# A decoder layer on one core: the recurrence in chunks of 64 tokens instead of 32

## The chip, the core and the metric

One NeuronCore of a Trainium2 chip runs the whole layer in one launch. The metric is device time in microseconds (us), the median of several executions. A profile is one execution, taken by the hardware profiler. Engines are called as the profile calls them: PE (TensorE, the matrix products; PEld its weight loads), DVE (VectorE), ACT (ScalarE), POOL (GpSimd) and SP (SyncE, which here issues most of the DMAs; ACT issues the others).

## What is computed

One hybrid layer on 2048 tokens of width 1024, all in float32. The token mixer has a projection, then two groups of heads: an RWKV-7 recurrence (8 heads of 64) and causal pooling; then an output projection, norms, and a gated MLP with a causal convolution. The part that the change rewrites is the recurrence:

```python
def step(state, inp):
    r_t, w_t, k_t, v_t, a_t, b_t = inp
    sa = jnp.einsum('bhvk,bhk->bhv', state, a_t)
    state = (state * w_t[:, :, None, :] + sa[..., None] * b_t[:, :, None, :]
             + v_t[..., None] * k_t[:, :, None, :])
    y_t = jnp.einsum('bhvk,bhk->bhv', state, r_t)
    return state, y_t
...
_, y = lax.scan(step, s0, seq)          # a = -kk, b = kk * alpha, per head 64 x 64 state
# then, per head: y = (y - mean) * rsqrt(var + eps) * ln_x_w + ln_x_b;  (y + bonus) * g
```

## The kernel before

The kernel has three phases. `phase_project` (lines up to L1020) forms the projection for four blocks of 512 tokens, scales r, k, a, b by the decay sums and stores them feature-major to scratch tensors in HBM; it also stores v and a token-major (`rows`, L899, sixteen 128x128 transposes a block, which `a_rows` at L609 copies and stores for a). In float32 it forms the grams of a and b inside chunks of C = 32 tokens and solves the inverse of (1 - strict gram) for two of the four blocks on DVE. `phase_recur` (L1024) runs the recurrence. `phase_out_and_ffn` and the output products do the rest of the layer.

`phase_recur` takes 128 tokens in an iteration `i`, from -2 to 19, with N = 16 groups of 128 tokens. It is a software pipeline written out by hand: `stages(i)` says which stages run in an iteration, `a1` for group i+2, `a2` for i+1, `b` for i, `o` for i-1, `c` for i-2, `d` for i-3. Each engine has its own `body(i, ...)`, whose order of instructions is the order in which that engine works; it stops at the first one whose semaphore isn't there. What stands in them:

- The chain, stage `b`, four times in an iteration, once for each chunk of 32 tokens: `from_state` (L1673, 4 products 128x64 by the state), ACT copies u from PSUM (`read_u`, L1402), `to_state` (L1681, 8 products), and DVE adds it to the state (`advance`, L1553; L1556 and L1559 in every second chunk, which also applies the decay `chunk_decay`). The next `from_state` waits for it.
- Preparation, `a1` and `a2`, for the groups to come: POOL builds `bk` from b and k (L1353, eight copies of 64x256, b and k interleaved and zeros between); `grams` (L1717, 32 products of 128x64); DVE masks them (`masks`, L1565, two instructions of 128x1024); `bk_transposes` (L1706, 16, copied by ACT at L1392); `z0_products` (L1729, 16 of 64x64), `w_products` (L1747, 32 of 32x32, from the inverse and from a token-major) and `z` (L1666, 16).
- Output, `o`: `from_r` (L1694, 32 products of 64x32) and `from_uv` (L1702, 32 of 128x32) into `ybank`, copied by ACT (L1472).
- Group norm, `c`: on DVE a sum, its scaling, a subtraction of the mean, the sum of squares, a reciprocal and a product (L1592, L1594, L1596, L1615, L1625, L1627); ACT squares (L1459) and takes the root (L1469). Stage `d`: four transposes (L1781), four scalings on ACT (L1446), bonus and gate on POOL (L1367, L1369), store.
- The inverses of the third and fourth block are solved in the gaps of DVE's order: `gap(0)` to `gap(7)` each take 2 to 4 small instructions (L1509, L1511), 27 parts a block over four iterations, the first part a mask of 128x1024 (L1500). This goes on in iterations 0 to 7 and is called solving below; iterations 8 to 15 have none of it.
- SP issues the loads of an iteration, 64 to 256 KB each: b and k, a and r, four of v, four of a, four of the inverse's 32x32 blocks (`spread`, L1222), bonus and gate.

PE has 228 products and transposes in a full iteration. Its order in it is: `from_state(0)`, `bk_transposes(0)`, `to_state(0)`, `from_r(0)`, the y transposes, `from_state(1)`, and so on to `w_products`, `grams` and `z`.

## Time and profile before

| what | value |
|---|---|
| median of 3 runs | 2328.89 us (2323.8 to 2330.03) |
| profiled execution, its span | 2329.1 us |
| PE busy | 2231.0 us, 96% |
| DVE, ACT, POOL busy | 1756.5, 1141.8, 1025.4 us |
| phase_project, first to last PE instruction | 0 to 541.6 us |
| phase_recur: first gram to `from_state(0)` of iteration 0 | 549.5 to 568.4 us |
| phase_recur: iterations 0 to 14 | 568.4 to 819.8 us |
| phase_recur: rest and change of phase | 819.8 to about 861 us |
| output products and MLP | about 861 to 2329 us |

A row of instructions reads: start, duration, engine, line of the kernel, operation, output<-input, shape, count, and in brackets how long the engine had been idle and for whom it waited. A float32 product is two records, so `x16` is eight products; a transpose is one record. "128*64 128x64" is a weight tile of 128 rows and 64 columns and an output of 64 columns moved through it.

### The profile page before, as it was taken

The page shows a single profiled execution, that of the slowest core. Times are in us where ns is not written, and L with a number is a line of the kernel's source. Part 1 is how long each engine was busy: PE and PEld are TensorE (multiplying, and loading weights), DVE is VectorE, ACT ScalarE, POOL GpSimd, SP SyncE. Part 2 cuts the span into 40 slices and gives each one's busy share as a digit, 9 for nine tenths or more (in the row PEclk, how much of TensorE's full clock was granted, in tenths as well). Part 3 has the DMA queues.
Part 4 walks back from the last instruction along what each step waited for, and adds up shares of the span by engine and source line. Part 5 has one row for each costly group of instructions (what it writes and reads, how often), then busy time and mean ns, then how long its engine had stood idle before and what let it go on. Part 6 is the DMA issues. An engine that isn't in the chain of part 4 may idle for free.

```text
span 2329.1 us, 43634 instructions
## 1 busy us (share of the span) xinstructions
PE 2231.0 (96%) x16652; PEld 1816.6 (78%) x16652; DVE 1756.5 (75%) x1910; ACT 1141.8 (49%) x1795; POOL 1025.4 (44%) x726
## 2 busy tenths in 40 slices
PE   7999999996999979998999999999999999999998
PEld 6777777775878768887888888788788888887886
DVE  3756798994884466769989999666799898976565
ACT  5646556452445554444444444454554444444543
POOL 4636466571234335535776766100146555541000
PEclk9999999998999989999999999999999999999999
DMA  7364556347567547895434343677733332326774
GB/s 203 93 227 134 178 160 209 106 140 216 154 166 194 144 144 234 268 279 166 153 119 147 121 146 128 217 252 255 237 119 115 104 111 93 113 95 202 247 260 145
DMA packets 435819, 395.61 MB, mean 170 GB/s; under 512 B 59548, under 2 KB 352076, under 8 KB 432332
## 3 DMA queue, kind: packets, MB, share of 16 engines
q1 hardware_dynamic: 407804, 343.06, 47.8%
q10 hardware_dynamic: 27856, 50.34, 6.0%
q8 instruction: 111, 1.82, 0.3%
q14 instruction: 48, 0.39, 0.1%
HBM read 266.97 MB, written 126.35 MB: 169 GB/s over the span
## 4 chain that ended last, share of the span: by engine, by line
PE 55%; DVE 3%; DMA 2%; ACT 1%; issue 1%; SPq 0%; ACTq 0%; POOLq 0%; POOL 0%; DVEq 0%
PE late_bank L133 18%; PE late_bank L134 18%; PE late_bank L135 18%; DVE wt_lo L2906 1%; DMA scratch_a<-p_keep 1%; ACT wt_hi L2727 1%; PE late_bank L2199 1%; DMA o_lo<-scratch_q 0%; DVE wt_lo L2860 0%; DMA p_keep<-in_w_down 0%; DMA raw<-in_w_down 0%; DMA scratch_x<-x_tile 0%; DMA p_keep<-scratch_td 0%; DVE p_ub L2869 0%; DVE x_tile L2168 0%
## 5 line engine op out<-in xcount | busy, mean ns | idle before, releaser
L133 PE MATMUL late_bank<-o_hi,wt_hi 128*128 128x512 f32 x1232 | 481.3, 391 | 8.0 <-DVE o_lo L2962 3.3
L134 PE MATMUL late_bank<-o_lo,wt_hi 128*128 128x512 f32 x1232 | 480.7, 390 | 0.0
L135 PE MATMUL late_bank<-o_hi,wt_lo 128*128 128x512 f32 x1232 | 480.6, 390 | 0.0
L431 POOL TENSOR_TENSOR p_w_lo<-p_w_raw,p_w_hi 128x1024 fp32r<-128x1024 f32 x72 | 190.4, 2645 | 221.2 <-ACT p_w_hi L502 221.2
L133 PEld LDWEIGHTS late_bank<-o_hi,wt_hi 128*128 128x128 f32 x1232 | 232.0, 188 | 58.7 <-issue 7.2
L135 PEld LDWEIGHTS late_bank<-o_hi,wt_lo 128*128 128x128 f32 x1232 | 232.1, 188 | 48.8
L134 PEld LDWEIGHTS late_bank<-o_lo,wt_hi 128*128 128x128 f32 x1232 | 232.0, 188 | 47.8
L2597 POOL TENSOR_TENSOR tsum<-raw 128x512 f32<-128x512 f32 x43 | 106.2, 2469 | 358.5 <-DVE p_ub L2947 179.4
L133 PE MATMUL p_ppr<-p_hT_hi,p_w_hi 128*128 128x512 f32 x576 | 233.4, 405 | 0.2 <-ACT p_ring L513 0.2
L133 PE MATMUL late_bank<-wt_hi 128*128 128x512 f32 x572 | 223.2, 390 | 7.2 <-DVE wt_lo L2906 6.6
L135 PE MATMUL p_ppr<-p_hT_hi,p_w_lo 128*128 128x512 f32 x576 | 226.6, 393 | 0.0
L134 PE MATMUL p_ppr<-p_hT_lo,p_w_hi 128*128 128x512 f32 x576 | 226.5, 393 | 0.0
L135 PE MATMUL late_bank<-wt_hi,wt_lo 128*128 128x512 f32 x572 | 222.6, 389 | 0.0
L134 PE MATMUL late_bank<-wt_lo,wt_hi 128*128 128x512 f32 x572 | 222.6, 389 | 0.0
L2674 ACT ACTIVATE wt_hi<-tsum 128x512 fp32r<-128x512 f32 x172 | 107.4, 627 | 169.3 <-PE late_bank L135 165.2
L2906 DVE TENSOR_TENSOR wt_lo<-raw,wt_hi 128x1024 fp32r<-128x1024 f32 x96 | 121.3, 1265 | 90.9 <-ACT wt_hi L2727 90.5
L2869 DVE TENSOR_TENSOR p_ub<-late_bank,p_ub 128x512 f32<-128x512 f32 x220 | 150.2, 683 | 34.6 <-PE late_bank L135 33.3
L2860 DVE TENSOR_TENSOR wt_lo<-raw,wt_hi 128x512 fp32r<-128x512 f32 x130 | 153.5, 1181 | 28.8 <-ACT wt_hi L2674 28.7
L2727 ACT ACTIVATE wt_hi<-raw 128x1024 fp32r<-128x1024 f32 x96 | 101.6, 1061 | 116.0 <-PE late_bank L135 96.9
L2860 DVE TENSOR_TENSOR wt_lo<-tsum,wt_hi 128x512 fp32r<-128x512 f32 x173 | 153.3, 887 | 1.8 <-ACT wt_hi L2674 0.6
L133 PEld LDWEIGHTS p_ppr<-p_hT_hi,p_w_hi 128*128 128x128 f32 x576 | 109.2, 190 | 36.3 <-issue 12.7
L133 PEld LDWEIGHTS late_bank<-wt_hi 128*128 128x128 f32 x572 | 107.4, 188 | 32.4 <-issue 6.4
(328 smaller groups left out, 4679.3 us busy)
## 6 DMA issues: line engine op xcount, KB each, us to landing
raw<-in_w_up SPq DMA_DIRECT2D x88, 512.0 KB, 5.1
p_w_raw<-in_w_in SPq DMA_DIRECT2D x72, 512.0 KB, 3.9
scratch_a<-p_keep SPq DMA_DIRECT2D x22, 1280.0 KB, 4.5
raw<-scratch_a SPq DMA_DIRECT2D x96, 256.0 KB, 3.0
raw<-scratch_td SPq DMA_DIRECT2D x52, 256.0 KB, 3.7
p_keep<-scratch_a SPq DMA_DIRECT2D x47, 256.0 KB, 2.9
scratch_a<-p_keep SPq DMA_DIRECT2D x44, 256.0 KB, 2.0
raw<-in_w_down SPq DMA_DIRECT2D x44, 256.0 KB, 4.1
```

Of the source, the lines that this page charges most:

```text
L133: nc.tensor.matmul(out, lhs_hi, rhs_hi, start=start, stop=False, skip_group_check=again)
L134: nc.tensor.matmul(out, lhs_hi, rhs_lo, start=False, stop=False, skip_group_check=again)
L135: return nc.tensor.matmul(out, lhs_lo, rhs_hi, start=False, stop=stop, skip_group_check=again)
L431: nc.gpsimd.tensor_tensor(w_lo[i][:, :, :], w_raw[i][:, :, :], w_hi[i][:, :, :].bitcast(F32), ALU.subtract).then_inc(s_wl, 1)
L2199: last = nc.tensor.transpose(bank[:, 4 + 2 * p + k // 4, (k % 4) * P:(k % 4 + 1) * P], hx[p][:, k * P:(k + 1) * P], ident[:, :])
L2597: nc.gpsimd.tensor_tensor(T1, B12, B11, ALU.subtract).then_inc(s_t, 1)
L2674: nc.scalar.activation(wt_hi[:, ph, :, :], weights(p, ph), ACT.Copy).then_inc(s_uh, 1)
L2727: nc.scalar.activation(dn_hi[r], dn_raw[r], ACT.Copy).then_inc(s_dh, 1)
L2860: nc.vector.tensor_tensor(wt_lo[:, ph, :, :], weights(p, ph), wt_hi[:, ph, :, :].bitcast(F32), ALU.subtract).then_inc(s_ul, 1)
L2869: nc.vector.tensor_tensor(dst, bank[:, b, :], src, ALU.add).then_inc(s_cd, 1)
L2906: nc.vector.tensor_tensor(dn_lo[r], dn_raw[r], dn_hi[r].bitcast(F32), ALU.subtract).then_inc(s_dl, 1)
```

## The change

C stays 32 for the grams that are inverted, but the recurrence goes over chunks of L = 64 tokens, two in an iteration.

- A chunk's step becomes: `from_state` (8 products 64x64 onto p in PSUM, where `z` has put the part of v), ACT copies p in two halves of four heads (`take_p`), `inverse` (8 products 64x64 by the 64x64 inverse, two halves, each as its half of p is there), ACT copies u in two halves (`take_u`), `to_state` (8 products 128x64), `advance` (two DVE instructions of 128x256).
- The 64x64 inverse is put together from the two 32x32 blocks and a corner: X21 = X2 L21 X1. `corner_left` and `corner_right` are 16 products of 32x32 each; a DVE transpose of 32x512 (`x1u`) and three kinds of ACT copies (`take_corner`, `m1`, `x21`) go with them. `w_products`, `z0_products`, the token-major a and its loads are gone, and in `phase_project` `a_rows`, its transposes and stores.
- b and k are stored and loaded as one tensor (`bk`), a and r (`ar`), bonus and gate (`bg`) likewise; POOL's copies (L1353) and its memset go. In an iteration SP issues 17 loads instead of 18: four of `bk` in pieces of 256 bytes, `ar`, v, `bg`, and ten of the inverse.
- PE: 156 products and transposes in a full iteration: `from_state` 16, `grams` 16 (64x128, 128 columns), `inverse` 16, `from_r` 16, y 4, `to_state` 16, corners 32, `transposed` 8, `from_uv` 16, `z` 16.
- `grams(c2)` fill both gram banks, so `grams(1)` waits for DVE's masks of `grams(0)` (`masked`, two instructions, 64x512 and 128x512, for each c2).
- Group norm: the subtraction of the mean, the square and the product by the reciprocal root move to POOL, which then has five instructions of 128x512 an iteration in place of two and eight copies. The root moves to the end of ACT's order, behind `x21`.
- The inverses are solved in six gaps an iteration over five iterations a block (27 parts as before), so in iterations 0 to 9; iterations 4 and 9 have only gaps 0 to 2.

The core of the diff; first DVE's order:

```diff
+                    if c:
+                        n = i - 2
+                        dve.wait_ge(s_yr, ONE + n + 1)
+                        nc.vector.tensor_reduce(stat[p][:, 0, :], y[n % 3][:, :, :], AX.X, ALU.add).then_inc(s_gn, 1)
+                        dve.wait_ge(s_gn, ONE + n + 1)
+                        nc.vector.tensor_scalar(stat[p][:, 0, :], stat[p][:, 0, :], -1.0 / H, None, ALU.mult).then_inc(s_mean, 1)
                     if a2:
-                        masks(am[q], strict, 0, s_am)
+                        n = i + 1
+                        dve.wait_ge(s_xl[n % 2], ONE + (n // 2 + 1) * 160)
+                        if n:
+                            wait_full(dve, i - 1, "m1")
+                        nc.vector.transpose(x1u[:, :, :, :].rearrange("p c u s -> p (c u s)"), x1[n % 2][:, :, :, :].rearrange("p c u t -> p (c u t)")
+                                            ).then_inc(s_xu, 1)
                     gap(0)
+                    gap(1)
...
+                    if a2:
+                        masked(0)
                     if b:
                         advance(0)
                     if a2:
-                        masks(ark[slot], causal, C, s_gr)
-                    gap(1)
...
+                        masked(1)
...
+                    gap(2)
...
+                    if c:
+                        dve.wait_ge(s_sq, ONE + i - 1)
+                        nc.vector.tensor_reduce(stat[p][:, 1, :], y2[:, :, :], AX.X, ALU.add).then_inc(s_var, 1)
+                    gap(3)
+                    if b:
+                        if o:
+
+                            dve.wait_ge(s_yd, ONE + 3 * (i - 1) + 2)
+                        advance(1)
                     gap(4)
                     if c:
-                        dve.wait_ge(s_sq, ONE + i - 1)
-                        nc.vector.tensor_reduce(stat[:, 1, :], y2[:, :, :], AX.X, ALU.add).then_inc(s_var, 1)
+                        dve.wait_ge(s_sd, ONE + i - 1)
+                        nc.vector.reciprocal(stat[p][:, 3, :], stat[p][:, 2, :]).then_inc(s_rec, 1)
                     gap(5)
```

POOL's order, and the two steps that take p and u in halves:

```diff
+                    if c:
+                        n = i - 2
+                        gp.wait_ge(s_mean, ONE + n + 1)
+                        nc.gpsimd.tensor_tensor(y[n % 3][:, :, :], y[n % 3][:, :, :], stat[p][:, 0, :].unsqueeze(2).to_broadcast([P, HEADS, H]),
+                                                ALU.add).then_inc(s_yc, 1)
...
+                        nc.gpsimd.tensor_tensor(y2[:, :, :], y[n % 3][:, :, :], y[n % 3][:, :, :], ALU.mult).then_inc(s_sq, 1)
...
                     if d and i < N + 2:
...
+                    if c:
+                        n = i - 2
+                        gp.wait_ge(s_rec, ONE + n + 1)
+                        nc.gpsimd.tensor_tensor(y[n % 3][:, :, :], y[n % 3][:, :, :], stat[p][:, 3, :].unsqueeze(2).to_broadcast([P, HEADS, H]),
+                                                ALU.mult).then_inc(s_yc2, 1)
...
+                    def take_p(c2):
+
+                        act.wait_ge(s_as, ONE + i * 2 + c2 + 1)
+                        for h in range(2):
+                            nc.scalar.activation(pz[rows_of(c2), h * PAIRS:(h + 1) * PAIRS, :], pbank[rows_of(c2), h], ACT.Copy).then_inc(s_p, 1)
...
+                    def inverse(c2):
+                        if c2 == 0:
+                            wait_read(pe, i - 1, "x21")
+                        for h in range(2):
+                            pe.wait_ge(s_p, ONE + i * 4 + c2 * 2 + h + 1)
+                            for j in range(PAIRS):
+                                u = h * PAIRS + j
+                                last = nc.tensor.matmul(ubank[:, h, j, :], xt[now][rows_of(c2), u, :], pz[rows_of(c2), u, :],
+                                                        start=True, stop=True, skip_group_check=True)
+                            last.then_inc(s_xp, 1)
```

The new orders as a whole, a full iteration:

```
PE:   from_state(0) grams(0) inverse(0) from_r(0) y-transposes to_state(0) grams(1) from_r(1)
      from_state(1) corner_left inverse(1) transposed(0) transposed(1) to_state(1) from_uv z
      corner_right(0) corner_right(1)
ACT:  take_p(0) take_corner(0) take_u(0) mo x4 take_corner(1) take_p(1) m1 take_u(1) t0 t1 y
      x21 x2 root
POOL: y+mean, y*y, mo+bonus, mo*gate, y*(1/root)
```

## Rows read from the trace of the kernel before

**Rows 1.** By stage: us, busy PE, PEld, DVE, ACT, POOL, PEclk, DMA share, GB/s.
```profile
0.00:541.60 541.60, 513.89 (x3232) 391.13 (x3232) 392.62 (x396) 297.54 (x454) 300.96 (x200) 0.99 0.54 166
```
**Rows 2.** The same for iterations 2, 4, 9 and 0 to 14 summed.
```profile
602.16:617.04 14.88, 14.86 (x434) 12.94 (x433) 12.88 (x29) 8.37 (x17) 3.90 (x9) 1.00 0.45 117
632.46:653.12 20.66, 18.36 (x441) 15.96 (x437) 14.02 (x30) 8.60 (x20) 9.23 (x18) 0.83 0.72 200
720.92:738.42 17.50, 15.87 (x440) 13.55 (x436) 8.42 (x15) 8.60 (x20) 6.02 (x10) 1.00 0.69 188
sum 251.46, PE 232.31 PEld 200.52 DVE 164.50 ACT 123.69 POOL 80.13; mean PE 15.49 PEld 13.37 DVE 10.97 ACT 8.25 POOL 5.34
```
**Rows 3.** PE in order of time in iteration 3, five of its groups.
```profile
617.04 0.68 PE L1673 MATMUL late_bank<-p_st,p_w 128*64 128x64 f32 x8
617.65 0.66 PE L1706 MATMUL late_bank<-p_ident,first_bk 128*128 128x128 f32 x4
618.24 0.69 PE L1681 MATMUL late_bank<-p_uv,p_bkt 128*64 128x64 f32 x16
618.85 0.65 PE L1694 MATMUL late_bank<-p_st,p_ar 64*32 64x64 f32 x32
...
625.84 1.15 PE L1729 MATMUL late_bank<-p_uv,am 64*64 64x64 f32 x32
```
**Rows 4.** PE's groups in phase_project: count | busy us, mean ns.
```profile
L892 PE MATMUL p_pm<-p_um,p_wlora 64*128 64x512 f32 x64 | 15.9, 615 | 0.0
L884 PE MATMUL p_pm<-p_um,p_wgate 128*128 128x512 f32 x32 | 14.4, 592 | 0.0
```
**Rows 5.** ACT's groups in the recurrence, 568.4 to 820 us.
```profile
L1402 ACT ACTIVATE p_uv<-late_bank 64x256 f32<-64x256 f32 x60 | 22.7, 378 | 80.7 <-PE late_bank L1673 80.3
L1469 ACT ACTIVATE p_stat<-p_stat,p_geps 128x8 f32<-128x8 f32 x13 | 3.9, 302 | 2.6 <-DVE p_stat L1615 2.4
```
**Rows 6.** DVE's groups in the same stretch.
```profile
L1565 DVE TENSOR_TENSOR am<-late_bank,p_strict 128x1024 f32<-128x1024 f32 x15 | 18.4, 1225 | 17.3 <-PE late_bank L1717 17.1
...
L1592 DVE TENSOR_REDUCE p_stat<-p_y 128x8 f32<-128x512 f32 x13 | 8.9, 686 | 0.4
...
L1625 DVE RECIPROCAL p_stat<-p_stat 128x8 f32<-128x8 f32 x13 | 2.6, 196 | 0.1
```
**Rows 7.** DVE in order of time, three solving instructions of iteration 6.
```profile
678.57 0.38 DVE L1509 TENSOR_TENSOR p_prod<-p_inv 128x220 f32<-128x220 f32 x1
...
679.40 1.34 DVE L1509 TENSOR_TENSOR p_prod<-p_inv 128x210 f32<-128x210 f32 x1
680.78 1.32 DVE L1511 TENSOR_TENSOR p_inv<-p_inv,p_prod 128x210 f32<-128x210 f32 x1
```
**Rows 8.** POOL in order of time, at the same moment.
```profile
679.15 1.36 POOL L1367 TENSOR_TENSOR p_mo<-p_mo,p_bonus 128x512 f32<-128x512 f32 x1 [12.60 <-ACT p_bkt L1392]
680.59 1.28 POOL L1369 TENSOR_TENSOR p_mo<-p_mo,p_gate 128x512 f32<-128x512 f32 x1
```
**Rows 9.** PE in order of time, behind the longest wait of iteration 0.
```profile
573.96 1.07 PE L1673 MATMUL late_bank<-p_st,w 128*64 128x64 f32 x8 [3.70 <-DVE p_st L1553]
```
**Rows 10.** Two-microsecond stretches: us, PE busy, PEclk, DMA share, GB/s.
```profile
574.00:576.00 2.00, 2.00 (x13) 0.51 0.51 118
...
646.00:648.00 2.00, 2.00 (x35) 0.50 0.75 219
```
**Rows 11.** PE in order of time in phase_project, the transposes of a.
```profile
290.01 1.91 PE L899 MATMUL p_pm<-p_ident,p_dec 128*128 128x128 f32 x16
291.68 0.48 PE L133 MATMUL p_ppr<-p_hT_hi,p_w_hi 128*128 128x512 f32 x1
```
**Rows 12.** SP's queue in order of time, the first loads of blocks of the inverse.
```profile
566.69 7.21 SPq L1222 DMA_DIRECT2D xt<-scratch_inv  x12
```
**Rows 13.** DVE in order of time: first solving instruction; bonus of the last group.
```profile
572.22 1.22 DVE L1500 TENSOR_TENSOR p_inv<-p_inv,p_above 128x1024 f32<-128x1024 f32 x1 [3.51 <-DMA p_above<-in_consts]
...
855.02 0.69 DVE L1640 TENSOR_TENSOR first_bt<-first_bt,p_bonus 128x512 f32<-128x512 f32 x1 [2.85 <-DMA p_gate<-scratch_g]
```

More of the change, by code:

```diff
@@ L652, in _ @@
                             high_w(n + WB)
-                        if f == 1 and b > 0:
-                            a_rows(b - 1, [pm[:, g, :] for g in range(TT)])
                         if f == 2:
@@ L929, in small @@
                 def small(b, pair):
-                    if pair == 0 and b > 0:
-                        pe.wait_ge(s_abr, ONE + b)
-                        rows(dec, [pm[:, g, :] for g in range(TT)], s_atn)
                     if pair in (2, 3) and b > 0:
@@ L1687, in from_r, with from_state @@
-                    def from_r(h2):
-                        if h2 == 0:
+                    def from_state(c2):
+                        pe.wait_ge(s_z, ONE + i * 2 + c2 + 1)
+                        if i * 2 + c2:
+                            pe.wait_ge(s_sn, ONE + i * 2 + c2)
+                        else:
+                            pe.wait_ge(s_xz, ONE + BATCH + 1)
+                        for j in range(PAIRS):
+                            for h in range(2):
+                                last = nc.tensor.matmul(pbank[rows_of(c2), h, j, :], ar[now][half(h), j, 0, tokens(c2)],
+                                                        st[p][c2][half(h), j, :], start=False, stop=True, skip_group_check=True)
+                        last.then_inc(s_as, 1)
@@ new lines, in to_state @@
+                    def to_state(c2):
+                        wait_read(pe, i - 1, f"t{c2}")
+                        pe.wait_ge(s_u, ONE + i * 4 + c2 * 2 + 2)
+                        for j in range(PAIRS):
+                            for h in range(2):
+                                last = nc.tensor.matmul(sbank[half(h), j, :], bkt[p][:, c2, j * P + h * H:j * P + h * H + H],
+                                                        uv[now][:, c2, h * PAIRS + j, :], start=True, stop=True)
+                        last.then_inc(s_s, 1)
@@ L1689, in from_r @@
+                    def from_r(h):
+                        if h == 0:
                             pe.wait_ge(s_yr, ONE + i - 1)
                         else:
[L1691 removed]
+                            pe.wait_ge(s_yd, ONE + 3 * (i - 1) + 1)
                         for j in range(PAIRS):
[L1693 to L1695 removed]
@@ L1696, in from_r @@
-                        last.then_inc(s_yd if h2 else s_yh, 1)
+                            for c2 in range(2):
+                                last = nc.tensor.matmul(ybank[rows_of(c2), j * 2 + h, :], ar[old][half(h), j, 1, tokens(c2)],
+                                                        st[q][c2][half(h), j, :], start=h + j == 0, stop=True, skip_group_check=True)
+                        last.then_inc(s_yd, 1)
                     def from_uv():
+                        pe.wait_ge(s_gm, ONE + 4 * i)
@@ new lines, in from_uv, with place_of, transposed @@
+                        last.then_inc(s_yd, 1)
+                    def place_of(name):
+                        t, k = job(i, name)
+                        pe.wait_ge(s_read[t], ONE + k)
+                        return bank[:, ROT[t], :], s_full[t]
+                    def transposed(c2):
+                        at, full = place_of(f"t{c2}")
+                        for j in range(PAIRS):
+                            last = nc.tensor.transpose(at[:, j * P:(j + 1) * P], kinds[:, j, 2 * c2:2 * c2 + 2, :].rearrange("d m s -> d (m s)"), ident[:, :])
+                        last.then_inc(full, 1)
@@ new lines, in corner_right @@
+                    def corner_right(h):
+                        at, full = place_of("x21")
+                        if h == 0:
+                            wait_read(pe, i, "m1")
+                        else:
+                            pe.wait_ge(s_xh, ONE + i + 2)
+                        for j in range(PAIRS):
+                            for c2 in range(2):
+                                u = h * PAIRS + j
+                                last = nc.tensor.matmul(at[quad(c2, 0), u * C:(u + 1) * C], m1[quad(c2, h), j, :], xd[q][quad(c2, h), j, :],
+                                                        start=True, stop=True)
+                        last.then_inc(full if h else s_xh, 1)
```

753 lines of the change are left out of this document (311 added, 442 removed).

## The prediction

> **What bounds the kernel now.** I read the busy time by stage first. In `phase_project` PE works 514 of 541.6 us [rows 1], and behind the recurrence it is as full, so there only PE instructions taken away count, and the change takes sixteen transposes a block. Then the same view by iteration: an iteration of the recurrence takes 14.9 us where PE never waits and 251.46 / 15 = 16.8 us on average, of which PE works 15.5 [rows 2]. So PE bounds it, with 1.3 us of waits on top; DVE, at 11 us on average and 13 to 14 while the inverses are solved, is second. Last the order of time, for the price of each kind of product and for what happens when DVE and POOL read at once.
>
> **PE's work in an iteration.** Starts of neighbouring groups in [rows 3] give: four products of 64 columns, one after another in one tile, 617.65 - 617.04 = 0.61 us, 0.152 each; four transposes 0.59; eight products in two tiles beside each other 0.61, 0.076 each; sixteen 64x64 products 1.15 less the overlap of 0.07 that the other rows have, 0.068 each. Whether two tiles with the same columns and different rows also run side by side, as `from_state` and `grams` now want, is in [rows 4]: a record of 512 columns costs 15.9 / 64 = 0.248 us where 64-row tiles alternate and 14.4 / 32 = 0.450 in one whole tile. They do. So, new: `inverse` 16 products in a single tile at 0.152, 2.4 us; `from_state`, `from_r`, `to_state`, `from_uv`, `z`, 80 products at 0.072, 5.8; `grams` 16, twice the columns, at 0.14, 2.2 (0.28 if they ran singly); 12 transposes 1.8; corners 32, priced by the nearest, 64x32 products at 0.58 / 16 = 0.036 [rows 3], some 1.3. The sum is 13.5 us where it was 14.9. A third fewer products is a tenth less time, because the products that go were the ones that ran four abreast.
>
> **What no longer fits under PE.** The root of the group norm stands last on ACT, and DVE's reciprocal waits for it with everything behind it. Take T as the moment when `masked(0)` ends and `grams(1)` starts. PE's groups from there to `corner_right(1)` sum to 9.1 us. ACT then copies `x21`, two at 0.38, and takes the root, 0.30 [rows 5]; DVE's reciprocal is 0.20 [rows 6]. With 0.05 to 0.1 us for each hand-over this ends at T + 10.6. Behind it on DVE stand `gap(5)`, the sum 0.69 [rows 6], its scaling 0.2, the transpose of `x1` 0.65 (32x512; nearest the sum over 512 elements, between 0.3 and 0.7), `gap(0)`, `gap(1)` and `masked(0)`, two of 512 elements, half of 1.225 and a fixed part, 1.3 [rows 6]. PE meanwhile runs to `to_state(0)` and can start `grams(1)` at T + 13.7.
>
> Without solving: the scaling waits for POOL's product (below), so 10.6 + 0.7 + 0.85 + 0.65 + 1.3 = T + 14.1. I take 14.4, with a quarter of the waits that PE has now. That is 2.4 less than the mean of 16.8.
>
> With solving: the three gaps hold about 7 small instructions of 0.35, and they meet POOL. In [rows 7, 8] an instruction of 220 elements takes 0.38 us alone; the next two take 1.34 and 1.32, and each ends 0.2 us behind an instruction of POOL of 1.36 and 1.28 us. A two-input DVE instruction that comes while POOL reads waits until POOL is through. POOL now has five such instructions in a row, started by DVE's own reciprocal and scaling: the product meets `gap(5)`, and mean, square, bonus and gate meet the gaps 0 and 1. Counted out from T + 10.6: `gap(5)` 1.9 (one instruction free, one behind POOL), sum and scaling 0.9, four POOL instructions 3.0 to 8.3, of which each lets one DVE instruction by, a fifth in some, 8.7, `masked(0)` 1.3: T + 20.6. If POOL never got in the way, 10.6 + 5.2 = T + 15.8. I take 20.6, since the rows are of the very same instructions.
>
> The Trainium skill has this as a rule (SBUF — State Buffer, Who interferes with whom): a DVE instruction with two SBUF inputs and a GpSimd instruction that reads SBUF lock each other out for a whole instruction, while one with a single SBUF input is free. It speaks against this change and for 20.6; a reading in which the two share would give 15.8. The trace agrees with the rule: 1.34 against 0.38.
>
> **The clock.** PE then idles from T + 13.7 to 20.6. After 3.70 us of waiting [rows 9] PE came back at PEclk 0.51, 1.2 GHz in place of 2.4, and was there again in iteration 4 at 0.50 [rows 10]; the slow stretch lasted some 3.3 us in the first and 6 in the second. At half speed that costs 1.7 to 3 us of work; I take 1.95, in the stretch that leads to the root, so it adds to the period: 22.5 us in a solving iteration that follows another.
>
> **The sum.** Start: DVE's first solving instruction waits for `above` until 572.2 [rows 13]; SP now issues ten small loads instead of four, each 7.21 / 12 = 0.6 us [rows 12], with three fewer v, four fewer a and a few more of b and k ahead, so about 2 us later; then 1.2 + 0.4 + 0.6 and the masks: T(0) = 577.1, and iteration 1 starts at 586.3, as it does now (568.4 + 18.2 = 586.5). From there, T to T: 13.4 (iteration 0 to 1, no group norm yet), 14.6 (1 to 2, mean and square only), 20.6 (2 to 3), five of 22.5 (3 to 4 and 5 to 9), 21.3 (4 to 5, without `gap(5)`), 16.0 (9 to 10: 14.1 and the slow clock): 198.4. Four more at 14.4 make 256.0, so iteration 15 starts at 842.3, where it started at 568.4 + 251.5 = 819.8 [rows 2]: 22.5 us late.
>
> `phase_project`: the sixteen transposes take 291.68 - 290.01 = 1.67 us with no wait around [rows 11], three blocks of it on PE's path, -5.0; of the last block ACT's copies of a end the phase, about 1.0, since the gate's store behind them ends it. Both from -6 to 0 if the stores in pieces of 512 bytes land later (ACT only issues them; the next use of their tiles is a block later, which hides them; without that cover a store of 1 MB would cost PE up to its landing time). POOL's copies for the first `bk` are gone and cost nothing now, since ACT's last store is later than they. Tail: the wait of 2.85 us for the gate of the last group goes [rows 13], POOL gets three more instructions of 1.3 us for each of two groups there, with mean and product on the path; between -3 and +8, I take +1.
>
> SP: 17 loads an iteration at 0.4 to 0.6 us are about 9 us of its queue, hidden under 14; its wait for `x21` holds back only loads of two groups ahead. ACT sums to 8.7 us an iteration and is covered likewise.
>
> 2329.1 - 6 + 22.5 + 1 = 2346.6, in terms of the profiled execution, whose span is within 0.3 us of the median of 2328.9. I forecast 2346.
>
> **The rivals.** *POOL and DVE hardly meet.* For it: most of DVE's instructions beside POOL now (sums, masks) keep their time, and an alternation may fall kindly. Against it [rows 7, 8]. Six full solving steps of 15.8, one of 15.0, then 14.1: 151.9 in place of 198.4, and no slow clock at T(9): iteration 15 starts at 795.8, 24 us early; 2329.1 - 6 - 24 + 1 = 2300. Faster; it decides if a solving iteration stays under about 19 us. *They meet, but PE's clock holds or half of the meetings fall away:* without the clock 2346.6 - 7 x 1.95 = 2333; with half of the 4.8 us as well in seven steps, 2316. Between them about 2325. *The row halves don't run side by side* in `from_state` and `grams`, other banks or not: 16 x 0.08 + 16 x 0.14 = 3.5 us more in each iteration where PE is bound; six iterations, some 20 us, and 2 us of start, gives 2366. [rows 4] speak against it. *It doesn't do what it says:* 156 products for 228 is plain in the diff, but if the small products cost by the record and not by the tile, PE would need 15.5 x 156 / 228 = 10.6 us; the chain through the root would still hold 14.1, so the time stays that of the others.
>
> **How the numbers follow.** Forecast 2346: 0.5. Hardly meet, 2300: 0.2. Clock holds or half the meetings, about 2316 to 2333: 0.22. Row halves singly, 2366: 0.08. The bounds of the forecast itself are -12 (slow stretches of 1.7 and less, DVE with exactly four instructions in the two gaps, no tail) and +15 (slow stretches of 3 us, tail +8). The range 2303 to 2362 leaves out some of the first rival and most of the last. A measurement here tells 0.3%, 7 us, from no change: faster (under 2322) 0.2 + 0.1 and a little of the forecast's low end, 0.32; same 0.14; slower (over 2336) 0.54.
>
> **What would show it.** Right: iterations 3 to 9 at 20 us and more and 10 to 14 at 14 to 15; in the first, DVE's solving instructions of 1.3 us beside POOL, PE's wait before `grams(1)` released by DVE's mask, 6 us long, and PEclk near 0.8 as a mean; `phase_project` 5 us shorter. Wrong: solving iterations near 16 us; a wait of PE that ends on a load or on ACT's copies of p; `inverse` at other than 1.2 us for eight products; or iterations 10 to 14 above 16 us, when the chain through p and u and not PE or the root would be the bound.

## The result and the profile after

The changed kernel takes 2376.3 us (median of 4, 2372.1 to 2378.4) beside 2329.5 for the kernel before: a ratio of 1.0186, 95% interval 1.0157 to 1.0216. Slower, as forecast, but 30 us above the 2346 of the prediction and above the 2362 at which its range ends. The profiled execution has a span of 2370.2 us, 41.1 more than before; the sum of the prediction was 2346.6 in those terms, so 23.6 us are missing from it. Three moments of the trace divide the miss: the start of iteration 1 (PE's first `from_state`), the start of iteration 15, and the first work of ACT in phase 3.

| stretch | before | predicted | after | miss |
|---|---|---|---|---|
| up to iteration 1 | 586.5 | 580.3 | 601.2 | +20.9 |
| iteration 1 to 15 | 233.3 | 256.0 | 250.1 | -5.9 |
| iteration 15 to phase 3 | 41.6 | 42.6 | 49.9 | +7.3 |
| phase 3 to the end | 1467.6 | 1467.6 | 1469.1 | +1.4 |

(Before: 568.4 + 18.2, 819.83 and 861.47 on its clock; after: 601.16, 851.24, 901.12.)

The first miss is in `phase_project`. The view by stage, which answers [rows 1] (columns: us, busy PE, PEld, DVE, ACT, POOL, PEclk, DMA share, GB/s), and the view of waits over the same stretch (us in total, times, longest):

```profile
0.00:558.40 558.40, 510.30 (x3168) 384.42 (x3168) 398.26 (x400) 289.54 (x438) 291.96 (x191) 0.96 0.54 155
```
```profile
ACT p_pin L511 <- issue: 47.2, 8, 9.9
...
PE p_ptr L958 <- DVE p_hT_lo L695: 27.5, 4, 9.3
```

PE has 64 instructions less and is busy for 3.6 us less, yet the stage is 16.8 us longer: PE waits 9.2, 9.3 and 8.2 us at the three boundaries between blocks. ACT and then PE in order of time at the third of them say what they did meanwhile:

```profile
402.76 6.44 ACTq L516 DMA_DIRECT2D scratch_bk<-p_alpha  x1
409.30 0.22 ACT L511 ACTIVATE p_pin<-p_pin 128x16 f32<-128x16 f32 x1 [8.38 <-issue]
...
409.64 3.35 ACTq L516 DMA_DIRECT2D scratch_ar<-p_dec  x1
...
414.78 1.26 ACT L629 ACTIVATE p_hT_hi<-p_ptr,p_gain 128x512 fp32r<-128x512 f32 x2
```
```profile
416.30 1.12 PE L958 MATMUL p_ptr<-p_ident,x_block 128*128 128x128 f32 x4 [8.16 <-DVE p_hT_lo L695]
```

ACTq is ACT's own sequencer giving out a DMA. While it gives out the store of b, for 6.44 us here and 7.8 in the last block, ACT does nothing else. DVE's `p_hT_lo` (at 415.50, after 10.94 us of waiting) comes behind ACT's `p_hT_hi`, which stands behind both issues, and PE waits for DVE. In the kernel before the same two stores of a block took 1.4 and 1.3 us (first line of each pair before, second after; min/median/max in ns over the four blocks):

```profile
L523 ACTq DMA_DIRECT2D scratch_bt<-p_alpha x4: 1382/1410/1466, 130.6 to 521.5; - x4
L523 ACTq DMA_DIRECT2D scratch_at<-p_dec x4: 1200/1272/1786, 132.4 to 523.8; - x4
```
```profile
L516 ACTq DMA_DIRECT2D scratch_bk<-p_alpha x4: 6213/6512/7800, 130.6 to 535.9; - x4
L516 ACTq DMA_DIRECT2D scratch_ar<-p_dec x4: 3350/4426/4671, 137.2 to 544.0; - x4
```

The recurrence looks as forecast. By iteration, with the columns of [rows 2], iterations 2, 7 and 10:

```profile
614.01:632.84 18.83, 16.11 (x301) 14.56 (x296) 12.07 (x24) 6.37 (x16) 2.25 (x2) 0.73 0.52 126
...
717.77:741.88 24.11, 16.78 (x305) 15.10 (x300) 15.83 (x27) 8.13 (x21) 5.97 (x5) 0.72 0.43 121
...
782.85:795.94 13.09, 12.68 (x306) 11.32 (x301) 6.92 (x13) 8.03 (x21) 5.67 (x5) 1.00 0.85 214
```

From iteration 2 to 9, while DVE solves, an iteration takes 17 to 24 us at a granted clock of 0.7 to 0.9; iterations 10 to 13, which don't solve, take 13.1 to 13.7 at 1.00. Iteration 14 takes 15.4 at 0.89, without a wait of PE over 0.7 us; what lowers its clock stays open. DVE in order of time in iteration 7, then POOL and PE in the same stretch, shows the collision and the wait:

```profile
719.07 0.20 DVE L1556 RECIPROCAL p_stat<-p_stat 128x8 f32<-128x8 f32 x1 [2.75 <-ACT p_stat L1428]
...
724.33 1.35 DVE L1456 TENSOR_TENSOR prod<-solve 128x238 f32<-128x238 f32 x1
...
727.10 0.41 DVE L1456 TENSOR_TENSOR prod<-solve 128x240 f32<-128x240 f32 x1
...
728.71 0.69 DVE L1501 TENSOR_TENSOR ark<-late_bank,p_causal 128x512 f32<-128x512 f32 x1
```
```profile
724.00 1.42 POOL L1317 TENSOR_TENSOR p_mo<-p_mo,p_bg 128x512 f32<-128x512 f32 x1
725.50 1.31 POOL L1319 TENSOR_TENSOR p_mo<-p_mo,p_bg 128x512 f32<-128x512 f32 x1
```
```profile
729.46 2.08 PE L1650 MATMUL late_bank<-first_ar,first_bk 64*128 64x128 f32 x16 [7.17 <-DVE ark L1501]
```

This is [rows 7, 8] again: 0.41 us alone, 1.35 when POOL reads. PE waits 7.17 us for the second product of `masked(0)` and comes back at half speed: `grams(1)` takes 2.08 us, where 1.16 is its time at 2.4 GHz.

Behind iteration 15 PE waits for POOL's scaling of y:

```profile
877.37 0.66 PE L1693 MATMUL late_bank<-p_ident,p_y 128*128 128x128 f32 x4 [1.75 <-POOL p_y L1323]
881.89 0.50 PE L133 MATMUL late_bank<-w_hi,m_hi 128*128 128x512 f32 x1 [1.10 <-POOL w_lo L1311]
887.32 1.11 PE L1693 MATMUL late_bank<-p_ident,p_y 128*128 128x128 f32 x4 [3.77 <-POOL p_y L1323]
```

### The profile page after: what moved, and what is told of

Read it like the earlier page. It is cut to its first block, busy times and chain, and to the rows that moved or that the text cites. A ratio compares the mean times of both kernels' runs of the same rounds, so it can differ in the third digit from the quotient of the medians.

```text
span 2370.2 us, 39095 instructions
## 1 busy us (share of the span) xinstructions
PE 2212.9 (93%) x14412; PEld 1803.8 (76%) x14412; DVE 1752.8 (74%) x1891; ACT 1124.0 (47%) x1795; POOL 1016.9 (43%) x645
## 4 chain that ended last, share of the span: by engine, by line
PE 53%; DVE 4%; DMA 2%; ACT 2%; issue 1%; SPq 0%; ACTq 0%; POOLq 0%; POOL 0%; DVEq 0%
PE late_bank L133 17%; PE late_bank L134 17%; PE late_bank L135 17%; DMA scratch_a<-p_keep 1%; DVE wt_lo L2866 1%; PE late_bank L2159 1%; ACT wt_hi L2687 1%; DMA o_lo<-scratch_q 0%; DMA p_keep<-in_w_down 0%; ACT late_bank L2705 0%; DMA raw<-in_w_down 0%; DVE wt_lo L2820 0%; DVE p_ub L2900 0%; DMA raw<-in_w_up 0%; DMA p_keep<-scratch_td 0%
## 5 line engine op out<-in xcount | busy, mean ns | idle before, releaser
L2820 DVE TENSOR_TENSOR wt_lo<-raw,wt_hi 128x512 fp32r<-128x512 f32 x130 | 151.9, 1168 | 29.2 <-ACT wt_hi L2634 29.1
## 6 DMA issues: line engine op xcount, KB each, us to landing
raw<-scratch_a SPq DMA_DIRECT2D x96, 256.0 KB, 3.0
raw<-scratch_td SPq DMA_DIRECT2D x52, 256.0 KB, 3.6
p_keep<-scratch_a SPq DMA_DIRECT2D x47, 256.0 KB, 3.1
scratch_a<-p_keep SPq DMA_DIRECT2D x44, 256.0 KB, 2.0
raw<-in_w_down SPq DMA_DIRECT2D x44, 256.0 KB, 4.3
```

What stands on the lines that cost most here:

```text
L2820: nc.vector.tensor_tensor(wt_lo[:, ph, :, :], weights(p, ph), wt_hi[:, ph, :, :].bitcast(F32), ALU.subtract).then_inc(s_ul, 1)
```

## The experiments

Four theories. A: `phase_project` loses its time where ACT stands at the issue of stores in small pieces; against it B (something else at the block boundary), C (the small packets load the DMA engines, whoever issues them) and that it needed the rest of the change. D: a solving iteration is long because the root comes last, two gaps that meet POOL stand between it and `masked(0)`, and the clock falls behind PE's wait; against it E (DVE is full wherever the gaps stand, or the chain through p and u binds) and F (loads). G: the tail hangs on the order of POOL's queue; against it H (it hangs on loads, stores and `w_lo`, whatever that order). All ratios are to the kernel before, timed again beside each group of kernels, where its median lay between 2327.7 and 2332.5 us. The differences in us below are of the medians in the table; by the ratios they would come out up to 5 us apart from that (55 us for 59, 26 for 28). The last two columns are the trace's: iterations 1 to 10, and iteration 15 to phase 3.

| kernel | us | ratio, 95% interval | it. 1-10 | tail |
|---|---|---|---|---|
| before | 2329.5 | 1 | 151.9 | 41.6 |
| after | 2376.3 | 1.0186 (1.0157-1.0216) | 181.7 | 49.9 |
| e1_layout | 2348.0 | 1.0074 (1.0052-1.0096) | 183.0 | 51.4 |
| e2_spq | 2349.7 | 1.0083 (1.0052-1.0114) | 182.8 | 49.8 |
| e3_gaps_late | 2317.5 | 0.9952 (0.9933-0.9970) | 129.8 | 49.0 |
| e4_unsolved | 2322.6 | one run | 126.5 | 50.6 |
| e5_both | 2294.4 | 0.9845 (0.9793-0.9897) | 133.4 | 50.0 |
| e6_norm_dve | 2374.2 | 1.0162 (1.0117-1.0208) | 180.0 | 44.8 |
| e7_root_first | 2349.5 | 1.0069 (1.0044-1.0095) | 162.4 | 49.1 |
| e8_both_tail | 2297.7 | 0.9839 (0.9800-0.9879) | 128.9 | 52.4 |
| e9_whole | 2306.1 | 0.9895 (0.9870-0.9921) | 143.2 | 51.9 |
| e10_best | 2291.4 | 0.9829 (0.9802-0.9855) | 133.4 | 43.4 |
| e11_before_pieces | 2353.4 | 1.0111 (1.0083-1.0139) | - | - |
| e12_pool_tiny | 2334.7 | 1.0019 (1.0001-1.0037) | 152.0 | 37.2 |

**The stores, another layout.** The scratch copies keep their pairs, but the tokens of a block lie together:

```diff
-    scr = {k: scratch(k, (BLOCKS, P, PAIRS, TT, 2, SC)) for k in ("ar", "bg", "bk")}
+    scr = {k: scratch(k, (BLOCKS, P, PAIRS, 2, TT, SC)) for k in ("ar", "bg", "bk")}
```

> The changed kernel with the scratch copies of b, k, a, r, bonus and gate laid out so that the stores of phase_project go in pieces of 2 KB again and the loads of phase_recur in pieces of 512 bytes or less; the number of instructions is the same. Theory A (my miss in phase_project): ACT's own queue stands still while it issues stores in pieces of 512 bytes (6.5 us for b, 4.4 for a, 1.4 for the bonus, where the kernel before took 1.4, 1.3 and 0.6), 9 us at the end of each block, and PE then waits for ACT and DVE. The issues fall back to 0.6, 1.4 and 1.3 us, the last wait of PE in phase_project ends near 538 to 542 us instead of 558, and the time falls by 15 to 20 us, to 2356 to 2361. Rival B: the stores only show what is late anyway, and PE waits at the block boundaries for something else that the change brought (the order of PE's instructions without the transposes of a, or the read of the a-b grams put into the middle of the next block's transposes): then the time falls by 3 us or less and the waits of 9 us stay.

28 us less, more than the 15 to 20 expected. ACT's issues are those of the kernel before, PE's waits at the boundaries fell from 27.5 to 5.9 us, and the stage ends at 530.3, 11.3 earlier than in the kernel before:

```profile
L516 ACTq DMA_DIRECT2D scratch_bk<-p_alpha x4: 1384/1440/1465, 131.3 to 512.7; - x4
L516 ACTq DMA_DIRECT2D scratch_ar<-p_dec x4: 1195/1268/1478, 133.1 to 515.2; - x4
```
```profile
0.00:530.30 530.30, 504.33 (x3168) 381.43 (x3168) 393.64 (x398) 289.94 (x438) 292.14 (x191) 1.00 0.53 163
```

Here PE is busy for 504.3 us at a clock of 1.00, where after it was 510.3 at 0.96: the lower clock had cost some 6 us on top of the waits.

**The same stores from another queue.**

```diff
-                            store("bk", 0, alpha[:, :, :], b, s_btst)
...
+                def store_b(b):
+                    sp.wait_ge(s_bt, ONE + b + 1)
+                    sp.dma_start(kind("bk", b, 0), tokens(alpha[:, :, :])).then_inc(s_btst, 16)
```

> The changed kernel with its layout kept, pieces of 512 bytes, but the stores of b and a issued by SP, at its steps 1 and 4 of the next block, instead of ACT. Theory A: what costs is that ACT itself stands at the issue; SP has nothing urgent behind them but weight loads, so the time falls as with the other layout, by 13 to 20 us, and a slow issue may show on SP instead. Rival C: what costs is the load of 2048 small packets a store on the DMA engines, whoever issues them, through late weight tiles: then little or nothing is won, under 5 us, and ACT waits for w_raw in place of standing at the issue.

26.5 us less, nearly all of it, with every packet as small as before: theory C falls. And the issue of b is short on SP. The very store that held ACT for 6.5 us takes SP 0.58, with no other store just ahead of it in the queue; that of a takes up to 2.5:

```profile
L339 SPq DMA_DIRECT2D scratch_bk<-p_alpha x4: 518/584/607, 115.4 to 497.5; - x4
L343 SPq DMA_DIRECT2D scratch_ar<-p_dec x4: 513/1758/2494, 153.6 to 504.1; - x4
```

**The same pieces in the kernel before.** Its six copies are padded so that a store goes in pieces of 512 bytes:

```diff
-    scr = {k: scratch(k, (P, PAIRS, SEQ)) for k in ("rt", "at", "bt", "kt", "bonus", "g")}
+    scr = {k: scratch(k, (P, PAIRS, SEQ // SC, 2, SC))[:, :, :, 0, :] for k in ("rt", "at", "bt", "kt", "bonus", "g")}
```

> The kernel before with one thing changed: its six scratch copies laid out so that the stores of phase_project go in pieces of 512 bytes, as in the changed kernel; the products, the norm and the recurrence stay. Theory A: ACT's issue of the b store goes from 1.4 to 6 to 8 us and that of a from 1.3 to 3.4 to 4.7, PE waits some 9 us at each block boundary, and the time rises by what the other layout gave back in the changed kernel, 28 us (20 to 30): 2349 to 2360. Rival: the cost needed the changed kernel's other edits (the a-b grams' read in the middle of the transposes), then it rises by under 8 us.

22 to 24 us more than the kernel before, with b's issue at 6.3 us and PE's waits for `p_hT_lo` at 26.9, where they were 5.9:

```profile
L523 ACTq DMA_DIRECT2D scratch_bt<-p_alpha x4: 6250/6274/6475, 131.5 to 539.1; - x4
```

Theory A is shown from both kernels, and B falls. The cost belongs to the layout of the stores, as long as ACT issues them, and to nothing else of the change.

**Two gaps behind the masks.** One thing is moved in DVE's order:

```diff
-                    gap(0)
-                    gap(1)
                     if a2:
                         masked(0)
                     if b:
                         advance(0)
                     if a2:
                         masked(1)
+                    gap(0)
+                    gap(1)
```

> The changed kernel with one thing moved: DVE's solving pieces gap(0) and gap(1) stand behind masked(1) instead of ahead of masked(0). Theory D (the prediction's, for the solving iterations): the root comes last on ACT, and behind it DVE has two gaps that meet POOL's four instructions before it gets to masked(0), for which PE waits 6 to 7 us and then comes back at half clock. With the gaps behind the masks that wait shrinks to 1 to 2 us and the clock holds: iterations 2 to 9 take 15 to 17 us instead of 17 to 24, in all 35 to 45 us less, 2331 to 2341. Rival E: DVE is simply full in a solving iteration (its own work and collisions wherever the gaps stand), or the chain through p and u holds the period near 20: then the time falls by 10 us or less, and PE's wait turns up before to_state or from_state, ended by DVE's advance.

59 us less, where 35 to 45 were expected: faster than the kernel before. Iterations 6 and 8 of this kernel, then DVE in iteration 7:

```profile
667.86:682.36 14.50, 12.90 (x305) 11.42 (x301) 12.54 (x26) 8.02 (x21) 5.68 (x5) 1.00 0.88 225
...
697.47:711.70 14.23, 12.88 (x300) 11.43 (x301) 13.27 (x28) 7.77 (x21) 5.72 (x5) 1.00 0.70 191
```
```profile
687.56 0.69 DVE L1501 TENSOR_TENSOR ark<-late_bank,p_causal 128x512 f32<-128x512 f32 x1
688.17 0.41 DVE L1490 TENSOR_TENSOR p_sumst<-late_bank,p_st 128x256 f32<-128x256 f32 x1
688.62 1.47 DVE L1492 TENSOR_TENSOR p_st<-p_sumst,chunk_decay 128x256 f32<-128x256 f32 x1
...
691.45 0.39 DVE L1456 TENSOR_TENSOR prod<-solve 128x234 f32<-128x234 f32 x1
```

My estimate had left out that the move also takes the gaps out of POOL's way. POOL's run of four instructions starts with DVE's own scaling and lasts 5 us; in that time DVE now does the masks, which take 0.69 us beside POOL as without it, and only the state's scaling (two inputs in SBUF) still meets it, 1.47 in place of 0.42. PE's waits for the masks, over iterations 1 to 9, fell from 42.7 us in all to 7.4, and the clock holds but for one iteration.

**No solving at all.** This kernel leaves the inverses of the third and fourth block unsolved but for their first and last part.

```diff
+                        if 0 < part < PARTS - 1:
+                            return
```

> The changed kernel without the solving steps of the last two blocks' inverses in phase_recur (only the first mask and the diagonal are left; the result for those blocks is wrong). Theory D: solving together with its collisions and the clock is all that parts iterations 2 to 9 from 10 to 13, so each takes 13.1 to 13.7 us and the time falls by 55 to 65 us, to 2311 to 2321. Rival F: the loads of the inverses' places and the first groups (SP's queue, which falls behind in these iterations) hold them up as well; then some of them stay above 15 us, with PE waiting on a load.

53.7 us less, at the edge of the expectation, and no faster than the kernel above, which does solve. What is left are iteration 12, 16.8 us, in which PE stands for 2.17 us for no wait that the profile shows, and above all iteration 5, 18.7 us: the first mask of the next block's inverse still stands ahead of `masked(0)`, its operand comes late, and PE waits 2.94 us. F is right to that extent; that the rest is D rests on this one run and on the kernel above.

```profile
661.75 1.85 DVE L1447 TENSOR_TENSOR solve<-solve,above 128x1024 f32<-128x1024 f32 x1 [0.92 <-DMA solve<-scratch_ab]
```

**The root first.** ACT takes the root ahead of `x21`'s copies:

```diff
+                    if c:
+                        act.wait_ge(s_var, ONE + i - 1)
+                        nc.scalar.activation(stat[p][:, 2, :], stat[p][:, 1, :], ACT.Sqrt, scale=1.0 / H, bias=geps[:, 0:1]).then_inc(s_sd, 1)
                     if a2:
                         take("x21",
```

> The changed kernel with ACT's root taken ahead of its copies of x21 instead of behind them; nothing else moves. The prediction put the root last in the chain: DVE waits 2.7 to 3.7 us for it while its input has long been there. If that link is right, the reciprocal comes about 2 us earlier in each solving iteration and everything behind it too, the slow stretch included: 8 iterations by 2 us and up to 1 us of clock, 2353 to 2362. If the root isn't the link (DVE's gaps are full anyway, or POOL's scaling hides it), under 5 us.

26.8 us less, a little more than expected; DVE's waits for the root over iterations 1 to 9 fell from 20.0 us (7 times) to 5.9 (7). The root was the last link, as the prediction had it.

**The norm off POOL.** DVE subtracts the mean and scales, ACT squares; the gaps stay ahead of the masks (the edit swaps `nc.gpsimd.tensor_tensor` for `nc.vector.tensor_tensor` in two places and for an activation of Square in one).

> The changed kernel with the group norm's three products taken off POOL again: mean and scaling by DVE, the square by ACT; the solving pieces stay ahead of the masks. It parts the two halves of theory D: what POOL's meetings cost from what the mere place of the gaps costs. DVE gets two instructions of 0.7 us, 1.4 us an iteration, and the solving instructions of 1.1 to 1.35 us beside POOL's mean and square (two of the four in gaps 0 and 1, the first of gap 5) fall back to 0.4: some 2.5 to 3 us. If meetings are the larger part: iterations 3 to 9 shorter by 1.5 to 3 us with a shorter slow stretch, and the tail shorter by 3 to 8 us since POOL's queue there is three instructions shorter: 2350 to 2362. If place is the larger part, the gain in the iterations is nil (1.4 us more against 2.5 less, ahead of the masks all of it) and only the tail's is left: 2368 to 2374. Over 2376: the meetings cost nothing that matters.

2 us less, inside the interval of the changed kernel. Iterations 1 to 10 take 180.0 us where they took 181.7: what DVE saves in meetings it spends on its two new instructions, all ahead of the masks. The tail is 5.1 us shorter, but iterations 10 to 14 are 5.2 us longer, 73.6 where they took 68.4: there DVE has the two instructions more and no solving to be relieved of a meeting.

**POOL's instructions shrunk.** Each works on 8 elements, so this kernel leaves out nearly all of the mean, the square, the scaling, bonus and gate; for instance

```diff
-nc.gpsimd.tensor_tensor(y2[:, :, :], y[n % 3][:, :, :], y[n % 3][:, :, :], ALU.mult).then_inc(s_sq, 1)
+nc.gpsimd.tensor_tensor(y2[:, 0:1, 0:8], y[n % 3][:, 0:1, 0:8], y[n % 3][:, 0:1, 0:8], ALU.mult).then_inc(s_sq, 1)
```

> The changed kernel with POOL's five instructions of an iteration shrunk to 8 elements (mean, square, bonus, gate and scaling are left out but for a sliver, so the result is wrong); semaphores, DVE's program and its order stay, the gaps ahead of the masks included. It prices POOL's meetings alone. The prediction's term was 4.8 us in a solving iteration and nearly 2 us of clock behind it. Theory D with that term: DVE's solving instructions all fall to 0.2 to 0.42 us, PE's wait before grams(1) from 6 to 7 us to 2 to 3, solving iterations from 20 to 24 us to 15.5 to 18, and the tail loses 4 to 8 us: 2322 to 2340. Rival: place alone (two gaps of 3.2 us without any meeting still come ahead of the masks, and the root last): 2355 or more.

41.6 us less: 29.7 in iterations 1 to 10, 12.7 in the tail. Iterations 3 to 9 take 121.9 us (633.38 to 755.28) where they took 150.0, so POOL's meetings and the clock behind them cost 4.0 us each (DVE's waits for the root stay, 20.7 us in all, so it isn't a shorter norm). But 17.4 us each is still far from the 13.1 of iterations without solving; PE in two of them:

```profile
641.42 1.16 PE L1651 MATMUL late_bank<-first_ar,first_bk 64*128 64x128 f32 x16 [2.22 <-DVE p_ark L1502]
...
708.89 2.08 PE L1651 MATMUL late_bank<-first_ar,first_bk 64*128 64x128 f32 x16 [3.20 <-DVE ark L1502]
```

Two gaps of 0.4 us instructions alone still keep PE waiting, and behind a wait of 3.20 us it comes back at 1.2 GHz all the same (behind 2.22 it did not; nor did it behind the 2.94 of the kernel without solving). So of the 8.3 us that these iterations had over the plain ones about half was meetings, and the rest is place, again with its clock. The kernel with the late gaps, which loses both, takes 15.0 us for each of the same seven.

**Both edits together.** The other layout and the late gaps.

> The changed kernel with both edits that won alone: stores of phase_project in pieces of 2 KB, and DVE's solving pieces 0 and 1 behind the masks. If the two costs are independent, as theories A and D have it (one ends before the other begins), their gains add: 2376 - 28 - 59 = 2289, between 2284 and 2295, some 40 us under the kernel before. If one hid part of the other (the load of phase_recur's first groups, say), it comes out above 2300.

5 us above the sum of the two gains by the medians, and equal to it by the ratios, 0.9845 of the kernel before (0.9793 to 0.9897): as far as that interval tells, the two costs are independent.

**POOL's order in the tail.** From iteration 16 on the scaling stands behind the square (`if i >= N: scaled(i, p)` there, `if c and i < N:` at its old place).

> As the kernel with both edits, and in the last three iterations POOL scales y right behind the square instead of behind its part of w_lo and the bonus and gate products. Theory G for the tail (10 us longer than in the kernel before, where I had taken 1): the last y stands in POOL's queue behind three instructions of 2.1 to 2.4 us, and PE's turn_y waits 1.8 and 3.8 us for it. Then the last turn comes 4 to 9 us earlier: 2280 to 2285 if the other is at 2289. Rival H: the tail hangs on the loads and stores of mix and on w_lo, whatever POOL's order: within 2 us of the kernel with both edits, or longer because w_lo comes later.

Nothing gained. The scaling comes early, and PE now waits for what was pushed behind it:

```profile
811.89 0.79 PE L133 MATMUL late_bank<-w_hi,m_hi 128*128 128x512 f32 x1 [8.86 <-POOL w_lo L1319]
```

H is right in part and G in part: this other order only moves the wait. That POOL simply has too much to do there is what the shorter tails with less work on POOL speak for (44.8, 43.4 and 37.2 us).

**Copies in one piece.** This undoes the halves, on top of both edits:

```diff
-                        for h in range(2):
-                            nc.scalar.activation(pz[rows_of(c2), h * PAIRS:(h + 1) * PAIRS, :], pbank[rows_of(c2), h], ACT.Copy).then_inc(s_p, 1)
+                        nc.scalar.activation(pz[rows_of(c2), :, :].rearrange("p (h j) v -> p h j v", h=2), pbank[rows_of(c2)], ACT.Copy).then_inc(s_p, 2)
```

> As the kernel with both edits, but p and u leave PSUM in one copy of 512 elements each, behind all products, in place of two halves: this undoes the one part of the change that is about halves. In an iteration the chain through p, the inverse, u and the state's update runs twice. With halves ACT's second copy stands beside products of the first; whole, inverse(c) waits for a copy of 0.6 us instead of 0.38, and u's copy starts only when all eight products are done. If PE bounds the iterations, other groups cover it and nothing moves: 2292 to 2298. If the chain bounds (PE waits in the last iterations and in the first one of the phase, in the slow stretches, for ACT's copies), 0.4 to 0.8 us for each of the 32 chunks: 2305 to 2320.

11.7 us more than with the halves by the medians, but the intervals, 0.9870 to 0.9921 and 0.9793 to 0.9897, overlap, so the totals alone don't settle it. In the traces iterations 1 to 10 are 9.8 us longer. PE's waits for p, over iterations 0 to 15, with the halves and then without:

```profile
PE late_bank L1612 <- ACT p_pz L1346: 2.7, 3, 1.2
```
```profile
PE late_bank L1610 <- ACT p_pz L1345: 7.3, 24, 1.5
```

That is 4.6 us more. The largest differences are iterations 2, 3 and 11, which take 20.4, 20.5 and 19.5 us at a granted clock of 0.58, 0.67 and 0.74, where they took 16.4, 15.9 and 13.1 at 0.79, 1.00 and 1.00 with the halves; whether the copies bring that about isn't shown. Four of the five plain iterations, 13.4 to 13.8 us, are no longer than with the halves.

**The version that takes all of it.** Both edits, the root first, and from iteration 16 on the norm by DVE and ACT.

> The version that should beat both: 2 KB stores, gaps 0 and 1 behind the masks, ACT's root ahead of the copies of x21, and in the last iterations (from the 16th on) the norm's mean and scaling by DVE and its square by ACT, which leaves POOL its part of w_lo and the bonus and gate products. Root: in the kernel with both edits DVE waits 0.3 to 0.9 us an iteration for it, so up to 7 us. Tail: with the whole norm off POOL the tail took 44.8 us in place of 49.9, so 5 us. 2283 to 2290. If the root's place only moved the wait (x21's copies now hold up inverse or the next corner), the tail's 5 us alone: 2289 to 2292.

2291.4 us, 0.9829 of the kernel before (0.9802 to 0.9855). The tail is 6.6 us shorter than with both edits; the root's place shows no gain in the trace once the gaps stand behind the masks: iterations 1 to 10 take 133.4 us either way. Its median is 3 us under that of e5_both and the two intervals overlap widely, so only the tail's 6.6 us in the trace speak for it; the total doesn't separate the two.

## Why the prediction was wrong

**The stores: the step that failed.** The prediction set `phase_project` to "-5.0", "about 1.0" for its end, and "Both from -6 to 0 if the stores in pieces of 512 bytes land later (ACT only issues them; the next use of their tiles is a block later, which hides them)". What hides the landing doesn't hide the issue. ACT stands for 6.5 and 4.4 us a block where it stood for 1.4 and 1.3, ACT's part of the next block's input is behind that, and PE waits some 9 us at each boundary and then works at a lower clock. e1_layout, e2_spq and e11_before_pieces put the price at 22 to 28 us. The term put the end of the stage at 535.6 us (541.6 - 6) and it came at 558.4, 22.8 later; the start of the recurrence behind it took 42.8 us to iteration 1 for the 44.7 forecast, which leaves the 20.9. Without the stores the term was right in sign and too small: e1_layout starts iteration 1 at 575.7, where I had 580.3. The range ended at 0 for this term, 16.8 us too low, and that alone put the result outside it. The trace of before did hold a hint: the issues of b and a took 1.4 and 1.3 us, more than twice the others, right behind other stores.

The Trainium skill (DMA: Bandwidth & Descriptors, Issuing engines are not separate DMA queues) says that issuing from several engines saves only the sequencer's time for the issue, "which is usually small relative to the DMA itself". The mechanism agrees with e2_spq, which saved just that. The size doesn't: here the issue of b was 6.5 us of the 13.6 from issue to landing (medians of four), and it sat on the engine whose work PE waited for.

**The recurrence: right by mechanism, and by sum in part through luck.** 196.9 us from the first `grams(1)` to that of iteration 10 (590.64 to 787.54), where I had 198.4; iterations 4 to 9 between 16.9 and 24.1 against 21.3 and 22.5; four plain steps at 13.2 (787.54 to 840.50) where I had 14.4. e7_root_first shows the root as the last link, e3_gaps_late and e12_pool_tiny the two gaps and the meetings, and the clock is in every row. Single steps missed by more: T(2) to T(3) took 24.2 us for 20.6, T(4) to T(5) 17.0 for 21.3. Two sizes were off and offset each other: meetings and clock together cost 4.0 us an iteration where I took 4.8 and nearly 2; and what is left without meetings is 17.4, not the 15.8 on which the rival of 2300 stood. That rival had left out that PE still waits 1.5 to 3.2 us and loses the clock by some of it: without any meeting iterations 1 to 15 take 221.1 us (603.32 to 824.39), where the rival had 209.5. That PE bounds an iteration otherwise held as well: 12.7 us of work in 13.1, where I had counted 13.5. One sum on the record is wrong: the rival of the row halves, 2346.6 + 20 + 2, is 2369 and not 2366; nothing hangs on it, since its products ran side by side.

The rule of the Trainium skill (SBUF — State Buffer, Who interferes with whom) that the prediction weighed held for these instructions: 1.35 against 0.41 us for two SBUF inputs beside POOL, 0.69 for the masks, with one input from PSUM, beside POOL or not. That a single SBUF input is free was said too broadly: the section excepts the 2-port modes, which `tensor_scalar` can enter, and in the kernel before the scaling of 8 elements, usually 0.17 us, once took as long as POOL's instruction beside it:

```profile
842.70 2.35 DVE L1594 TENSOR_SCALAR p_stat<-p_stat 128x8 f32<-128x8 f32 x1
```
```profile
842.62 2.40 POOL L1361 TENSOR_TENSOR w_lo<-w_raw,w_hi 128x1024 fp32r<-128x1024 f32 x1 [1.29 <-ACT w_hi L1409]
```

**The halves** weren't priced at all. On top of both edits they are worth up to 11.7 us by the medians, of which the trace shows 4.6 as waits for p. What they give in the changed kernel itself, where DVE bounds the solving iterations, wasn't tried.

**The tail: a term of the right kind, mis-sized.** I took +1 out of -3 to +8 and counted POOL's new instructions at 1.3 us. It is +8.2. POOL's mean takes 1.95 us and its square 1.83 there, while DVE makes `m_lo` and `w_lo` at the same time, 1024 elements with both inputs in SBUF, and its own part of `w_lo` stands in the same queue:

```profile
866.58 1.95 POOL L1301 TENSOR_TENSOR p_y<-p_y,p_stat 128x512 f32<-128x512 f32 x1
...
868.67 1.83 POOL L1306 TENSOR_TENSOR p_squares<-p_y 128x512 f32<-128x512 f32 x1
870.46 2.39 POOL L1311 TENSOR_TENSOR w_lo<-w_raw,w_hi 128x1024 fp32r<-128x1024 f32 x1
```

The norm off POOL gives back 5.1 to 6.6 us of it, all of POOL's work 12.7. Which part of the last 1 to 3 us is the norm's longer chain in iteration 15 and which the loads stays open.

## What to carry to other kernels

A DMA's issue is an instruction of the engine that issues it: when a layout cuts a store into four times as many pieces, look at how long that engine's queue stands at it and who waits for its next work, and give the store to a queue that nobody waits for or lay the copy out the other way. In a list written by hand, work that can be late (here the solving pieces) belongs behind the instruction for which the next engine waits, above all if what releases it also starts the other engine's reads. And where a wait of some 3 us can cost the clock, a rival that takes the collisions away must still be costed with the wait that remains.

## What the hardware showed that I had not expected

The time of an issue was longer right behind other issues of the same queue: a store of 1 MB in pieces of 512 bytes took ACT 0.54 us (gate, alone), 1.4 (bonus, behind one other), 6.5 (b, behind two) and 4.4 (a, behind three), and SP 0.58 (b, with no store just ahead). On SP too the store of r in e2_spq took 0.52 to 0.55 us in three blocks and 1.59 in the last, behind a run of other issues. It isn't that the two queues stood in each other's way: at the second boundary of the changed kernel SP issued nothing between 264.64 and 284 us, while ACT stood at b for 6.58 us from 265.51. Whether the queue itself is full or the DMA engines behind it are wasn't separated. In a meeting POOL is slowed as well: 1.04 us for its mean alone, 1.95 beside DVE's subtraction of 1024 elements. And one move of two calls in DVE's list was worth 55 to 59 us, some 2.4% of the kernel, with not one instruction more or less.
